# Layer 0's second-block attention on one Trainium2 core: context and latent units taken in turns

## The chip, the cores and the metric

The kernel runs on one core of one Trainium2 chip. The metric is the device time of one execution, in microseconds (us). The engines are TensorE (PE; its weight loads are listed apart as PEld), VectorE (DVE), ScalarE (ACT), GpSimd (POOL) and SyncE (SP), which issues most of the DMAs. Before the change the median of three runs is 2735.27 us (2731.71 to 2745.95).

## The reference, cut to what matters

Two transformer blocks of two layers each follow one another. The change is in the second block, in its layer 0. There two streams of 256 tokens are processed, context and latent. Context queries see the 256 context keys; latent queries see 512 keys, those of the context and their own. In the last layer only the latent stream is needed.

```python
for i in range(DEPTH):
    last = i == DEPTH - 1
    qg_c, kg_c, vg_c, qm_c, km_c, vm_c, pool_c = mixer_inputs(hc, *layer_w, None)
    qg, kg, vg, qm, km, vm, pool_l = mixer_inputs(h, *layer_w, rope)
    mix = token_mix(qg, concat([kg_c, kg]), concat([vg_c, vg]),      # latent: 512 keys
                    qm, concat([km_c, km]), concat([vm_c, vm]), pool_l, ...)
    ...
    if not last:
        mix_c = token_mix(qg_c, kg_c, vg_c, qm_c, km_c, vm_c, pool_c, ...)   # context: 256 keys

def token_mix(qg, kg, vg, qm, km, vm, ...):
    og = attention(qg, kg, vg, HEAD_DIM ** -0.5)     # 6 heads, keys of 64 numbers, 2 key/value heads
    om = attention(qm, km, vm, MLA_QK ** -0.5)       # 6 heads, keys of 96 numbers
    return concat([merge_heads(og), merge_heads(om), op]) @ w_out

def attention(q, k, v, scale):                       # blocks of 128 queries
    p = softmax(einsum(q, k) * scale)
    return einsum(p, v)
```

## The kernel before, in words

Everything is written by hand: each engine has its own instruction list, and semaphores tie the lists together. There is no scheduler; the order of the code is the order on each engine.

The attention of the second block is cut into units. A unit is one stream, one head and one of two tiles of 128 queries, so layer 0 has 2 x 12 x 2 = 48 units and layer 1 has 24. `units(i)` lists them, and unit n of the list is what every engine means by n. In layer 0 the list holds the 24 units of the context stream first, and then the 24 of the latent stream. In each stream the first 12 units are of the heads with keys of 64 numbers (GQA below; their scores are L2463), the last 12 of those with 96 (MLA; L2465).

A unit runs through the engines like this:

- PE, `scores(n)`: one matmul of 128 queries against 256 keys (context) or 512 keys (latent), in float32. Score banks are four (`SCORE_BANKS`), taken in turns by n.
- DVE: the row maximum of the scores (L2925), and its negative, scaled (L2926).
- ACT: the exponential with the sum of each row (L2715).
- DVE: the reciprocal of that sum (L2932), and the product with the probabilities (L2933).
- PE, `turn(n)`: transposes of the probabilities, two pieces of 128 x 128 for a context unit and four for a latent one (L2477).
- ACT: the copy of the transposed probabilities out of the bank (L2724).
- PE, `attend(n)`: probabilities times values, two matmuls for a context unit and four for a latent one (L2494).
- DVE, after every fourth unit: four units (two heads, two tiles) fill one output bank, 6 or 7 in turns, and a copy brings it to `h` (L2939).

The work is staggered. In step n, PE issues `scores(n)`, `turn(n-2)` and `attend(n-3)`. ACT does the exponential of unit n and then the copy of unit n-2. DVE does the maximum of unit n, the normalisation of unit n-1, and where a group of four has ended at unit n-3, its copy. The first `attend` of a group waits (`av_out`) until the bank that it takes has been emptied by the copy of the group before the last.

Before the attention stand the projections of the MLA heads, whose last copies (L2705) the third unit's scores wait for. Behind it stands the output projection (L2515), whose first matmul waits for the last copy to `h`.

A line such as `128x256 f32 x2` in the profile is one float32 matmul: it shows as two records of PE.

Of the kernel before, what the change touches and what calls it, by code (L numbers as in the profile page):

```python
# [1894 lines left out]
GQ, KVH = 6, 2  # L1895
MH, NOPE, ROPE_D = 6, 64, 32
# [99 lines left out]
def build_second(nc, ctx, a, scratch, store, out):  # L1996
# [83 lines left out]
    def streams(i):  # L2080
        return (CTX, LAT) if i < DEPTH - 1 else (LAT,)
# [6 lines left out]
    def cols(s, t=0, n=T):  # L2088
        return slice(s * T + t, s * T + t + n)
# [8 lines left out]

    def units(i):

        return [(s, hd, t) for s in streams(i) for hd in range(GQ + MH) for t in range(2)]

    def layer_ends(i):
        for x in signals:
# [54 lines left out]
    def unit_base(i):  # L2159
        return len(units(0)) if i else 0  # L2160
# [45 lines left out]
    def tensor_program(pe):  # L2206
# [137 lines left out]
        for i in range(DEPTH):  # L2344
# [95 lines left out]
            for t in range(4):  # L2440
# [3 lines left out]
                last.then_inc(*((used_kv.sem, 1) if t == 3 else mla_done.up()))  # L2444

            us = units(i)

            def scores(n):
# [32 lines left out]
            def attend(n):  # L2481
                s, hd, t = us[n]
                if n == 0:
                    pe.wait_ge(*mla_evac.at(i, 2 * MH + 4))
                pe.wait_ge(*pt_ready.at(0, ub + n + 1))
                pair = n // 4
                if n % 4 == 0 and pair >= 2:
                    pe.wait_ge(*av_out.at(0, ub // 4 + pair - 1))
                hi = slice((hd % 2) * HD, (hd % 2 + 1) * HD)
                nk = (T if s == CTX else TT) // P  # L2490
                for k in range(nk):
                    kv = hd // (GQ // KVH)
                    v = vg[:, k, kv * HD:(kv + 1) * HD] if hd < GQ else vm[:, k, (hd - GQ) * HD:(hd - GQ + 1) * HD]
                    last = mm(ps[6 + pair % 2][hi, t * P:(t + 1) * P], v, probT[:, n % 2, k * P:(k + 1) * P],  # L2494
                              start=(k == 0), stop=(k == nk - 1))
                last.then_inc(*av_done.up())

            for n in range(len(us) + 3):
                if n < len(us):
                    scores(n)  # L2500
                if 2 <= n < len(us) + 2:
                    turn(n - 2)
                if n >= 3:
                    attend(n - 3)
# [41 lines left out]
    def scalar_program(act):  # L2546
# [69 lines left out]
        for i in range(DEPTH):  # L2616
# [82 lines left out]
            for t in range(4):  # L2699
# [5 lines left out]
                go(vm[:, t, :], ps[4 + t][:, 0:MH * HD], ACT.Copy).then_inc(*mla_evac.up())  # L2705

            us = units(i)
            for n in range(len(us) + 2):
                if n < len(us):
# [40 lines left out]
    def vector_program(dve):  # L2750
        v = nc.vector

        def step(i, instruction, signal):

            instruction.then_inc(*signal.up())
            dve.wait_ge(*signal.now(0))
# [83 lines left out]
        for i in range(DEPTH):  # L2840
# [78 lines left out]
            for n in range(len(us) + 3):  # L2919
                if n < len(us):  # L2920
                    s, hd, t = us[n]
                    nk = T if s == CTX else TT
                    dve.wait_ge(*sc_done.at(0, ub + n + 1))
                    m1 = smx[:, n % 4:n % 4 + 1]
                    step(0, v.tensor_reduce(m1, ps[SCORE_BANKS[n % 4]][:, 0:nk], AX_X, ALU.max), sm_max)  # L2925
                    v.tensor_scalar(m1, m1, -((HD if hd < GQ else MQK) ** -0.5), None, ALU.mult  # L2926
                                    ).then_inc(*sm_max.up())
                if 1 <= n <= len(us):
                    b = (n - 1) % 4
                    nk = T if us[n - 1][0] == CTX else TT  # L2930
                    dve.wait_ge(*sm_act.at(0, ub + n))
                    step(0, v.reciprocal(ssum[:, b:b + 1], ssum[:, b:b + 1]), sm_norm)  # L2932
                    v.tensor_scalar(prob[:, b, 0:nk], prob[:, b, 0:nk], ssum[:, b:b + 1], None,  # L2933
                                    ALU.mult).then_inc(*sm_norm.up())
                if n >= 3 and (n - 3) % 4 == 3:
                    s, hd, t = us[n - 3]
                    pair = (n - 3) // 4
                    dve.wait_ge(*av_done.at(0, ub + n - 2))
                    v.tensor_copy(h[:, hd // 2, cols(s)], ps[6 + pair % 2][:, 0:T]).then_inc(*av_out.up())  # L2939
            first_low(MlpTiles(i, streams(i)[0]))  # L2940
# [121 lines left out]
    @block.vector  # L3062
    def _(dve):
        nc.vector.memset(ones_row[:, 0:P], 1.0).then_inc(*placed.up())
        nc.vector.memset(ones_row[:, P:], 1.0).then_inc(relu_done.sem, 1)
        vector_program(dve)
# [33 lines left out]
```

## Time and profile before

| what | us |
|---|---|
| median of three runs | 2735.27 |
| lowest, highest run | 2731.71, 2745.95 |
| profiled execution | 2742.86 |
| its span from first to last instruction | 2740.9 |
| PE busy | 2630.0 (96%) |
| DVE busy | 1700.7 (62%) |
| ACT busy | 1028.4 (38%) |

The profile shows one execution. Its time is the span and 2 us around it. The shares are means over a span with many stages: PE is busy nearly all the time, and yet its time depends on the clock that it was granted and on what it works on. The attention of layer 0's second block stands at 1765 to 1883 us of the span. PEclk is the clock granted to TensorE, as a share of 2.4 GHz: 1.00 is 2.4 GHz and 0.50 is 1.2 GHz.

### The profile page before, as it was taken

What the parts mean: (1) busy time and instruction counts of PE and PEld (TensorE: products, weight loads), DVE (VectorE), ACT (ScalarE), POOL (GpSimd) and SP (SyncE); (2) the same over time, 40 slices, a digit from 0 to 9 for tenths busy, and PEclk for the clock granted to TensorE, in tenths of its full rate; (3) what the DMA queues carried; (4) which work ended last, traced back from release to release, by engine and by line L of the source; (5) the groups of instructions that cost most, each with busy time, mean ns of one, the idle gap of its engine ahead of it and who ended that gap; (6) DMA issues with size and microseconds to landing.
All of it is one profiled execution on the core that took longest, in us unless ns stands there. A gap on an engine that the chain in (4) does not pass through costs nothing. (4 is left out here: it accounts for less than half of the span.)

```text
span 2740.9 us, 44687 instructions
## 1 busy us (share of the span) xinstructions
PE 2630.0 (96%) x18787; PEld 2324.0 (85%) x18787; DVE 1700.7 (62%) x2283; ACT 1028.4 (38%) x1275; POOL 99.2 (4%) x179
## 2 busy tenths in 40 slices
PE   8999989999989999989999999999999999989999
PEld 7999888989989999779899954355799899737999
DVE  6887655768768877656678822553455455354555
ACT  4335302444343354204443321643333333264333
POOL 2110000001101100000001000000000000000000
PEclk9999989999999999989999999889999999999999
DMA  8775201647766764004557752100355555210452
GB/s 277 261 260 185 93 1 47 200 140 244 261 216 223 264 224 154 16 1 138 171 174 258 260 193 77 46 1 31 127 183 183 199 184 185 78 62 31 140 183 93
DMA packets 279510, 415.63 MB, mean 152 GB/s; under 512 B 10105, under 2 KB 235721, under 8 KB 277698
## 3 DMA queue, kind: packets, MB, share of 16 engines
q1 hardware_dynamic: 260332, 348.16, 38.5%
q0 software_dynamic: 18128, 64.20, 6.8%
q8 instruction: 112, 1.84, 0.3%
q10 hardware_dynamic: 902, 1.15, 0.1%
q14 instruction: 36, 0.29, 0.0%
HBM read 399.82 MB, written 13.65 MB: 151 GB/s over the span
## 5 line engine op out<-in xcount | busy, mean ns | idle before, releaser
L614 PE MATMUL ps<-h_high,w_high 128*128 128x256 f32 x1984 | 567.9, 286 | 17.5 <-DVE w_low L1407 10.5
L616 PE MATMUL ps<-h_high,w_low 128*128 128x256 f32 x2016 | 572.3, 284 | 0.0
L614 PEld LDWEIGHTS ps<-h_high,w_high 128*128 128x128 f32 x1984 | 382.8, 193 | 20.3 <-DVE w_low L1407 11.4
L616 PEld LDWEIGHTS ps<-h_high,w_low 128*128 128x128 f32 x2016 | 389.0, 193 | 0.0
L1407 DVE TENSOR_TENSOR w_low<-ring,w_high 128x2048 fp32r<-128x2048 f32 x132 | 302.3, 2290 | 138.5 <-ACT w_high L1150 138.2
L615 PE MATMUL ps<-h_low,w_high 128*128 128x256 f32 x1312 | 373.4, 285 | 0.0
L2797 DVE TENSOR_TENSOR w_low<-ring,w_high 128x2048 fp32r<-128x2048 f32 x96 | 220.0, 2292 | 240.6 <-ACT w_high L2581 240.4
L1150 ACT ACTIVATE w_high<-ring 128x2048 fp32r<-128x2048 f32 x132 | 252.3, 1915 | 266.7 <-DMA ring<-in_ffn_w_in 147.9
L2581 ACT ACTIVATE w_high<-ring 128x2048 fp32r<-128x2048 f32 x96 | 183.8, 1916 | 331.2 <-PE ps L2260 304.1
L615 PEld LDWEIGHTS ps<-h_low,w_high 128*128 128x128 f32 x1312 | 254.0, 194 | 0.0
L1428 DVE SCALAR_TENSOR_TENSOR mod_acc<-wmod,cond,mod_acc 128x512 f32<-128x512 f32 x336 | 230.8, 748 | 0.0
L2258 PE MATMUL ps<-h_high,w_high 128*128 128x256 f32 x768 | 218.3, 284 | 2.8 <-DVE h_low L2766 2.8
L2260 PE MATMUL ps<-h_high,w_low 128*128 128x256 f32 x768 | 218.1, 284 | 0.0
L2259 PE MATMUL ps<-h_low,w_high 128*128 128x256 f32 x768 | 218.0, 284 | 0.0
L2258 PE MATMUL ps<-act_high,w_high 128*128 128x256 f32 x768 | 217.5, 283 | 0.0
L2259 PE MATMUL ps<-act_low,w_high 128*128 128x256 f32 x768 | 217.3, 283 | 0.0
L2260 PE MATMUL ps<-act_high,w_low 128*128 128x256 f32 x768 | 217.3, 283 | 0.0
L614 PE MATMUL ps<-act_high,w_high 128*128 128x256 f32 x704 | 200.3, 285 | 0.0
L615 PE MATMUL ps<-act_low,w_high 128*128 128x256 f32 x704 | 199.5, 283 | 0.0
L616 PE MATMUL ps<-act_high,w_low 128*128 128x256 f32 x704 | 199.5, 283 | 0.0
L1383 DVE TENSOR_TENSOR w_low<-ring,w_high 128x2048 fp32r<-128x2048 f32 x64 | 146.3, 2291 | 81.6 <-ACT w_high L1097 80.8
L615 PE MATMUL ps<-w_high 128*128 128x256 f32 x544 | 153.9, 283 | 0.0
(426 smaller groups left out, 5395.0 us busy)
## 6 DMA issues: line engine op xcount, KB each, us to landing
ring<-in_w_mlp SPq DMA_DIRECT2D x96, 1024.0 KB, 5.5
ring<-in_ffn_w_in SPq DMA_DIRECT2D x88, 1024.0 KB, 8.8
wmod<-in_w_mod POOLq DMA_DIRECT2D x96, 512.0 KB, 6.3
ring<-in_ffn_w_out SPq DMA_DIRECT2D x44, 1024.0 KB, 5.1
ring<-in_w_mix_in SPq DMA_DIRECT2D x26, 1024.0 KB, 5.5
ring<-in_xattn_w_kv SPq DMA_DIRECT2D x16, 1024.0 KB, 5.3
mod_scratch<-mod_acc POOLq DMA_DIRECT2D x24, 512.0 KB, 5.5
ring<-mod_scratch SPq DMA_DIRECT2D x12, 1024.0 KB, 6.8
```

Source lines behind the costliest of these rows:

```text
L614: mm(dst, w_hi, x_hi, start=start, stop=False, **more)
L615: mm(dst, w_hi, x_lo, start=False, stop=False, **more)
L616: return mm(dst, w_lo, x_hi, start=False, stop=stop, **more)
L1150: go(w_high[buffer], ring[:, tiles.slot(r, b), :], ACT.Copy).then_inc(w_high_ready.sem, 1)
L1383: v.tensor_tensor(w_low[:, n % RING, :], slot(n), w_high[COLUMN_HIGHS[c]], ALU.subtract).then_inc(*column_low.up())
L1407: v.tensor_tensor(w_low[:, slot, :], ring[:, slot, :], w_high[buffer], ALU.subtract).then_inc(w_low_ready.sem, 1)
L1428: v.scalar_tensor_tensor(mod_acc[:, c, :], w, col, mod_acc[:, c, :], ALU.mult, ALU.add).then_inc(mod_step.sem, 1)
L2258: mm(dst, w_hi, x_hi, start=start, stop=False, **more)
L2259: mm(dst, w_hi, x_lo, start=False, stop=False, **more)
L2260: return mm(dst, w_lo, x_hi, start=False, stop=stop, **more)
L2581: go(w_high[parity], ring[:, tiles.slot(r, q), :], ACT.Copy).then_inc(w_high_ready.sem, 1)
L2797: v.tensor_tensor(w_low[:, slot, :], ring[:, slot, :], w_high[parity], ALU.subtract).then_inc(w_low_ready.sem, 1)
```

## The change

`units(i)` now runs over heads and tiles outside and over the streams inside. In layer 0 the list becomes context, latent, context, latent, and so on: unit 0 is the context's first tile of head 0, unit 1 the latent's. Four units of one stream still share an output bank, but they are now every other unit: groups end at units 8g+6 (context) and 8g+7 (latent). The context's groups always take bank 6 and the latent's bank 7. Layer 1 has one stream, and its order and its banks come out as before.

```diff
     def units(i):
 
-        return [(s, hd, t) for s in streams(i) for hd in range(GQ + MH) for t in range(2)]
+        return [(s, hd, t) for hd in range(GQ + MH) for t in range(2) for s in streams(i)]
+
+    def group_of(i, n):
+
+        both = len(streams(i))
+        return n // (4 * both) * both + n % both
+
+    def first_of_group(i, n):
+        return n % (4 * len(streams(i))) < len(streams(i))
+
+    def last_of_group(i, n):
+        both = len(streams(i))
+        return n % (4 * both) >= 3 * both
...
-                pair = n // 4
-                if n % 4 == 0 and pair >= 2:
+                pair = group_of(i, n)
+                if first_of_group(i, n) and pair >= 2:
                     pe.wait_ge(*av_out.at(0, ub // 4 + pair - 1))
...
-                if n >= 3 and (n - 3) % 4 == 3:
+                if n >= 3 and last_of_group(i, n - 3):
                     s, hd, t = us[n - 3]
-                    pair = (n - 3) // 4
+                    pair = group_of(i, n - 3)
                     dve.wait_ge(*av_done.at(0, ub + n - 2))
                     v.tensor_copy(h[:, hd // 2, cols(s)], ps[6 + pair % 2][:, 0:T]).then_inc(*av_out.up())
```

The lines below are instructions in the order of their engine: line, operation, output and inputs, size, and how many in a row. The lines of the changed kernel are 12 higher. First TensorE in the GQA part. Before, among the context's units:

```order
L2463 MATMUL ps<-qk 128x256
L2477 MATMUL ps<-consts_sb,prob 128x128 x2
L2494 MATMUL ps<-probT,vg 64x128 x2
L2463 MATMUL ps<-qk 128x256
L2477 MATMUL ps<-consts_sb,prob 128x128 x2
L2494 MATMUL ps<-probT,vg 64x128 x2
```

and among the latent's, 60 rows on:

```order
L2463 MATMUL ps<-qk 128x512
L2477 MATMUL ps<-consts_sb,prob 128x128 x4
L2494 MATMUL ps<-probT,vg 64x128 x4
L2463 MATMUL ps<-qk 128x512
L2477 MATMUL ps<-consts_sb,prob 128x128 x4
L2494 MATMUL ps<-probT,vg 64x128 x4
```

After the change, in the same part:

```order
L2475 MATMUL ps<-qk 128x512
L2489 MATMUL ps<-consts_sb,prob 128x128 x4
L2506 MATMUL ps<-probT,vg 64x128 x2
L2475 MATMUL ps<-qk 128x256
L2489 MATMUL ps<-consts_sb,prob 128x128 x2
L2506 MATMUL ps<-probT,vg 64x128 x4
L2475 MATMUL ps<-qk 128x512
L2489 MATMUL ps<-consts_sb,prob 128x128 x4
L2506 MATMUL ps<-probT,vg 64x128 x2
```

A unit's own work is the same; its neighbours are not. Between two scores now stand the turn of the unit of the same stream two places back and the attend of the other stream: 4 transposes with 2 matmuls, then 2 transposes with 4 matmuls.

Then VectorE around the copies to `h`. Before, among the context's units:

```order
L2933 TENSOR_SCALAR prob<-prob,ssum 128x256
L2925 TENSOR_REDUCE smx<-ps 128x1
L2926 TENSOR_SCALAR smx<-smx 128x1
L2932 RECIPROCAL ssum<-ssum 128x1
L2933 TENSOR_SCALAR prob<-prob,ssum 128x256
L2939 COPY h_sb<-ps 128x256
L2925 TENSOR_REDUCE smx<-ps 128x1
```

After the change:

```order
L2945 TENSOR_SCALAR prob<-prob,ssum 128x256
L2951 COPY h_sb<-ps 128x256
L2937 TENSOR_REDUCE smx<-ps 128x1
L2938 TENSOR_SCALAR smx<-smx 128x1
L2944 RECIPROCAL ssum<-ssum 128x1
L2945 TENSOR_SCALAR prob<-prob,ssum 128x512
L2951 COPY h_sb<-ps 128x256
L2937 TENSOR_REDUCE smx<-ps 128x1
L2938 TENSOR_SCALAR smx<-smx 128x1
```

Two copies now come in consecutive steps, once in eight units, where one came in every fourth. Normalisations of 256 and of 512 columns take turns.

## Rows read from the trace of the kernel before

**Rows 1.** the page, busy time of the engines

```profile
PE 2630.0 (96%) x18787; PEld 2324.0 (85%) x18787; DVE 1700.7 (62%) x2283; ACT 1028.4 (38%) x1275; POOL 99.2 (4%) x179
```

**Rows 2.** stretches of layer 0: us, busy by engine, PEclk, DMA share, GB/s

```profile
1764.57:1767.99 3.42, 1.80 (x10) 0.93 (x9) 2.07 (x9) 1.58 (x5) 0.00 (x0) 1.00 0.47 123
1767.99:1808.94 40.95, 40.95 (x121) 23.54 (x120) 16.74 (x65) 13.26 (x48) 0.00 (x0) 0.50 0.04 16
```

**Rows 3.** timeline (start us, us, engine, line, names, shape), first units

```profile
1764.87 0.48 PE L2463 MATMUL ps<-qk 64*128 64x256 f32 x1
...
1770.76 1.22 PE L2463 MATMUL ps<-qk 64*128 64x256 f32 x2
```

**Rows 4.** timeline, one GQA context unit at the low clock

```profile
1784.83 1.22 PE L2463 MATMUL ps<-ksw,qk 64*128 64x256 f32 x2
...
1785.97 0.69 PE L2477 MATMUL ps<-consts_sb,prob 128*128 128x128 f32 x2
...
1786.59 1.12 PE L2494 MATMUL ps<-probT,vg 128*64 128x128 f32 x4
...
1787.64 1.22 PE L2463 MATMUL ps<-qk 64*128 64x256 f32 x2
```

**Rows 5.** timeline, scores of two MLA context units at the low clock

```profile
1801.13 1.22 PE L2465 MATMUL ps<-km,qm 96*128 96x256 f32 x2
...
1803.76 1.22 PE L2465 MATMUL ps<-km,qm 96*128 96x256 f32 x2
```

**Rows 6.** timeline, MLA context units at the full clock

```profile
1811.87 0.70 PE L2465 MATMUL ps<-km,qm 96*128 96x256 f32 x2
...
1812.60 0.43 DVE L2925 TENSOR_REDUCE smx<-ps 128x1 f32<-128x256 f32 x1 [0.36 <-PE ps L2465]
...
1813.25 0.48 ACT L2715 ACTIVATE prob<-ps,smx 128x256 f32<-128x256 f32 x1 [0.59 <-DVE smx L2926]
...
1813.72 0.38 ACT L2724 ACTIVATE probT<-ps 128x256 f32<-128x256 f32 x1
...
1814.14 0.41 PEld L2494 LDWEIGHTS ps<-probT,vm 128*64 128x64 f32 x4 [0.17 <-ACT probT L2724]
...
1814.73 0.70 PE L2465 MATMUL ps<-km,qm 96*128 96x256 f32 x2
...
1816.45 0.42 DVE L2939 COPY h_sb<-ps 128x256 f32<-128x256 f32 x1
```

**Rows 7.** timeline, GQA latent units at the full clock

```profile
1829.12 1.12 PE L2463 MATMUL ps<-qk 64*128 64x512 f32 x2
...
1830.28 0.69 DVE L2925 TENSOR_REDUCE smx<-ps 128x1 f32<-128x512 f32 x1 [1.18 <-PE ps L2463]
...
1830.76 1.09 PE L2494 MATMUL ps<-probT,vg 128*64 128x128 f32 x8
...
1831.20 0.69 ACT L2715 ACTIVATE prob<-ps,smx 128x512 f32<-128x512 f32 x1 [1.39 <-DVE smx L2926]
...
1831.78 0.29 PEld L2463 LDWEIGHTS ps<-qk 64*128 64x128 f32 x2 [0.17 <-issue]
...
1831.88 0.59 ACT L2724 ACTIVATE probT<-ps 128x512 f32<-128x512 f32 x1
```

**Rows 8.** timeline, the last latent score and the first output projection

```profile
1875.36 1.12 PE L2465 MATMUL ps<-km,qm 96*128 96x512 f32 x2
...
1882.83 5.42 PE L2515 MATMUL ps<-h_sb,ring 128*128 128x512 f32 x12 [0.52 <-DVE h_sb L2939]
```

**Rows 9.** busy us by stretch, layer 1's attention, latent units only

```profile
2454.07:2457.48 3.41, 3.41 (x13) 2.54 (x13) 1.36 (x4) 1.45 (x4) 0.00 (x0) 0.50 0.00 0
```

**Rows 10.** timeline, layer 1, a latent unit at the low clock

```profile
2453.92 1.03 PE L2477 MATMUL ps<-consts_sb,prob 128*128 128x128 f32 x4
...
2454.88 1.97 PE L2494 MATMUL ps<-probT,vg 128*64 128x128 f32 x8
...
2456.78 1.45 PE L2463 MATMUL ps<-qk 64*128 64x512 f32 x2
```

## The prediction

> **What bounds the kernel now.** I read the page's busy times first [rows 1]. PE is busy in 96% of the span, so only what changes PE's time, or makes it idle, can move the end much. DVE and ACT have room.
>
> Then I read the busy time by stretch around the changed place, which is where this case is decided [rows 2]. From 1767.99 to 1808.94 us PE is busy all the time and has a granted clock of 0.50, that is 1.2 GHz. Before that it had 1.00 for 3.42 us in which it was busy for only 1.80 us, waiting for the first softmax. The low clock covers all the GQA units of the context after the first three and about six of its MLA units; behind 1808.94 the remaining context units and the latent ones run at about half these durations [rows 6, 7].
>
> The timeline then gives what a unit costs at each clock. A step of the stagger is score, turn, attend.
>
> - Context, GQA, low clock: 1784.83 to 1787.64 = 2.81 us, of which the score is 1.14, the turn 0.62, the attend 1.05 [rows 4]. PE has no gap.
> - Context, MLA, low clock: 1801.13 to 1803.76 = 2.63 us [rows 5].
> - Context, full clock: 1811.87 to 1814.73 is two units, 1.43 us each [rows 6]. Here PE isn't the only bound: its attend (1814.14) starts when ACT's copy ends (1813.72 + 0.38), and the row names that copy as what released it.
> - Latent, GQA, full clock: 1829.12 to 1831.78 = 2.66 us, attend 1.02 [rows 7].
>
> The whole stretch, from the first score (1764.87 [rows 3]) to the first output projection (1882.83 [rows 8]), takes 117.96 us. About 21 us of it are the low clock's: some 10 GQA units at 2.81 - 1.43 and 6 MLA units at 2.63 - 1.43.
>
> **The change part by part.** No instruction is added or removed; the work of each engine in the stretch is the same. Three things change.
>
> *The output banks.* Each stream now has one bank, so the first attend of a group waits for the copy of the same stream's last group, which ended two units earlier, instead of a group back. DVE makes that copy in the step in which the attend is done, and PE's turn of the next step already waits for a later instruction of DVE, the normalisation. The copy is 0.42 us [rows 6] and lies beside the next score, the shortest of which at full clock (context) keeps DVE waiting longer than that. Cost 0. If the cover were gone it would be 6 groups x 2 streams x 0.42 = 5 us at the very most; I keep nothing below 0.
>
> *The latency of a latent unit at full clock.* PE may issue the score of a latent unit when the attend of the latent unit two places back in the list is over. Followed along the rows [rows 7]: score to maximum 1830.28 - 1829.12 = 1.16; maximum to exponential 0.92; exponential to the copy behind it 0.68; copy to attend 0.59 and 0.04 to 0.05 of semaphore (as 1813.72 + 0.38 to 1814.14 [rows 6]); attend to the next score 1.02. Together 4.42 us. That chain spans two units of the list. Before, two latent units took 2 x 2.66 = 5.32 us of PE, so it was hidden. Now the two are a latent and a context unit, with 2.66 + 1.43 = 4.09 us, so the chain sets the pace: a pair takes 4.42 us, 0.33 more. Could the pair take less than 4.09? A context unit's own chain (2.86 for two units [rows 6]) is now well hidden, and PE's own work in one is perhaps 0.1 to 0.15 below 1.43; this would count only if the latent chain were not there, so the bounds for a pair are 3.95 and 4.42, and I take 4.42, since it is a sum of rows.
>
> *The low clock.* This is the large term. The first steps still wait for the first softmax, with little on PE, as before [rows 2]; I take it that the clock falls there again. Then it matters how long it stays down. What the rows show: with context GQA units alone it never came back, though PE had no gap. With context MLA units alone it came back after about six. In layer 1, with latent units alone, it was low for a mere 3.41 us [rows 9], in which PE did little but a turn of four transposes and an attend of eight records, up to 2456.78 [rows 10]. In the new order each run of turn and attend between two scores is 0.62 + 1.90 us (context turn, latent attend: 2456.78 - 2454.88) or about 1.05 + 1.05. That is between the context's 1.67 and the latent's 2.9, and each run is fenced by scores over only 64 rows, as the context's GQA units were. So the two neighbours bound it: back at once, or not before the MLA units. I take the second, because the runs here are broken by such scores as often as before and half of them are nearly the context's own length; it is a close choice. In the MLA part, where context units alone sufficed, I let the clock come back within the first pair.
>
> A page of the Trainium skill says the opposite. "TensorE: Matmul & The Clock Gate", in the part on the clock gate, has it that sustained matmul activity releases the throttle, and that only idle gaps bring it back. By that rule the busy PE of the new order gets its clock back quickly, which is the second case below. The trace disagrees with the rule as it stands: 40.95 us busy in a stretch of 40.95 us, at 0.50 [rows 2].
>
> The price at the low clock. Latent GQA unit: attend 1.90 [rows 10]; four matmuls more than a context attend cost 0.85, so 0.21 a record; the turn is then 0.62 + 2 x 0.21 = 1.05 (the row has 0.96, partly at full clock); the score has 256 columns more in each of two records, and at 0.21 for 128 columns of one pass pair that is 4 x 0.21 more, 2.00. Together 4.95 (bounds: 4.3 with the score row's 1.45 as it stands, 5.32 as twice the full-clock unit). A pair is 2.81 + 4.95 = 7.76.
>
> The sum:
> - first score to unit 4: before 1770.76 - 1764.87 = 5.89 [rows 3]; now two of the four scores are latent (+0.43 at full clock, 1.16 against 1812.60 - 1811.87; +0.85 at the low) and a turn has four pieces (+0.43): 7.6
> - ten more GQA pairs at 7.76: 77.6
> - first MLA pair, midway between 2.63 + 4.8 at the low clock and 4.42: 5.9
> - ten MLA pairs at 4.42: 44.2
> - the last pair to its latent score, half a pair: 2.1 (DVE and ACT work ahead there)
> - last latent score to the output projection, as before: 1882.83 - 1875.36 = 7.5 [rows 8]
>
> Total 144.9 against 117.96, or +26.9 us. In the terms of the profiled execution that is 2742.9 + 26.9 = 2769.8. This execution is 7.6 us above the median of 2735.27, and the trace doesn't say where. If the 7.6 is a longer low stretch among the context's MLA units, it isn't carried over (the new order is at the low clock there whatever comes later); if it lies elsewhere, it is, and the median would be 2762. I take 2767.
>
> What lies behind the stretch isn't moved: the output projection starts from a full bank of weights in either case, and the DMAs are idle in this stretch (share 0.04 [rows 2]), so nothing new is late.
>
> **The rivals.**
>
> *B, the clock comes back within the first GQA pairs* (not slower). The place is the first latent attend next to a context turn at about 1775 us. Layer 1 speaks for it [rows 9, 10], and the skill's rule; the 25 us of context GQA units that PE filled without it speak against. With one pair at the low clock behind the start: 7.6 + 7.8 + 20 x 4.42 + 2.1 + 7.5 = 113.4, 4.6 less than before; each further low pair adds 3.3. In the profiled execution's terms 2738, by the median 2731 to 2740; I call it 2735. It changes sign against my forecast from the point where fewer than about three pairs are low.
>
> *A2, it comes back somewhere in the middle of the GQA part.* Nothing in the trace excludes it, and the runs of before spread over 14 us. With 4 to 8 low pairs behind the start it is 2745 to 2760.
>
> *C, the clock doesn't fall at all at the start.* 5.9 + 21 x 4.42 + 2.1 + 7.5 = 108.3, so -9.7: 2733 in the profiled execution's terms, 2726 by the median. Against it: the first steps have even more waiting, since the first normalisation is behind a maximum of 512 columns, and layer 1's start lost the clock too [rows 9].
>
> *D, it stays low through the MLA part too.* Ten more pairs at 2.63 + 4.8 instead of 4.42, and the end at the low clock: some 36 us more, 2800 or above. The context MLA units that got it back alone speak against.
>
> *E, the order gains as PE work.* The latent chain is shorter than I sum it, no clock is lost, and a pair costs 3.95: 5.9 + 21 x 3.95 + 9.6 = 98.5, -19.5, about 2720. Nothing in the rows supports both halves at once.
>
> *That the change does nothing* would need the pace of a pair to be the sum of both and the same low stretch; its time lies within B's.
>
> **How the numbers follow.** A 0.50, A2 0.10, B 0.25, C 0.05, D 0.05, E 0.05. The likeliest is A, 2767, with a range of its own of 2758 to 2776 (the price of a low latent unit, and the 7.6 us). The range over the cases runs from 2730 to 2776: it leaves out D, E, most of C and the edges of B and A. A measurement of this kernel can tell about 0.5% from no change, here 13.7 us. Slower by more: A, D and most of A2, 0.63. Faster by more: E and a little of B and C, 0.06. Within: 0.31.
>
> **What would show it.** The granted clock in the stretch behind 1768 us: 0.50 for some 85 us is A, under 20 us is B. The distance between two latent scores: 7.8 us at the low clock, 4.4 at the full. At the full clock the latent attend must be released by ACT's copy (L2736), with PE idle about 0.3 us before it; if its distance is 4.1 and nothing waits, my chain is wrong. DVE's copies to `h` must come in twos with no attend waiting for them. Layer 1's attention should be as before. A clock at 1.00 from the first units on would make the prediction wrong whatever the pace.

## The result, and the profile after

| | before | after |
|---|---|---|
| median of the runs, us | 2740.61 (four runs, 2731.71 to 2746.12) | 2770.93 (four runs, 2769.91 to 2772.32) |
| ratio to before | 1 | 1.0108 (95%: 1.0082 to 1.0135) |
| span of the profiled execution, us | 2740.9 | 2767.9 |
| first score to first output projection in layer 0, us | 117.97 | 144.57 |

The kernel became 1.1% slower in these executions; three of twelve later ones didn't lose this time (last experiment). Of the 27.0 us between the two spans, 26.6 lie in the changed stretch. Here are the busy times and the stretches of the profile after, with the columns of [rows 1, 2]:

```profile
PE 2652.7 (96%) x18787; PEld 2333.8 (84%) x18787; DVE 1700.4 (61%) x2283; ACT 1027.2 (37%) x1275; POOL 99.2 (4%) x179
```

```profile
1763.61:1767.02 3.41, 2.32 (x8) 1.13 (x8) 2.06 (x7) 1.69 (x5) 0.00 (x0) 1.00 0.40 136
1767.02:1852.35 85.33, 85.33 (x244) 47.49 (x244) 29.00 (x96) 24.15 (x71) 0.00 (x0) 0.50 0.02 7
1852.35:1907.80 55.45, 50.15 (x280) 32.03 (x278) 31.02 (x101) 26.30 (x72) 0.00 (x0) 1.00 0.00 1
```

The instruction counts are those of before, and PE is busy for 23 us more with the same work. The middle row says why: 85.33 us without a gap at a granted clock of 0.50 (1.2 GHz), where before had 40.95 [rows 2]. Behind it, at the full clock, PE is idle for 5.3 of 55.45 us.

A pair is a latent and a context unit. The next view is TensorE's timeline of one GQA pair at the low clock, in the kernel after, with one line left out: from a latent score over a context score to the next latent one.

```profile
1783.03 2.07 PE L2475 MATMUL ps<-ksw,qk 64*128 64x512 f32 x2
...
1786.07 1.12 PE L2506 MATMUL ps<-probT,vg 128*64 128x128 f32 x4
1787.12 1.22 PE L2475 MATMUL ps<-qk 64*128 64x256 f32 x2
1788.27 0.69 PE L2489 MATMUL ps<-consts_sb,prob 128*128 128x128 f32 x2
1788.89 1.97 PE L2506 MATMUL ps<-probT,vg 128*64 128x128 f32 x8
1790.79 1.22 PE L2475 MATMUL ps<-qk 64*128 64x512 f32 x1
```

1783.03 to 1790.79 is 7.76 us. The next view is an MLA pair at the full clock, with lines of all engines, many left out:

```profile
1865.79 1.13 PE L2477 MATMUL ps<-km,qm 96*128 96x512 f32 x2
...
1866.95 0.69 DVE L2937 TENSOR_REDUCE smx<-ps 128x1 f32<-128x512 f32 x1 [1.56 <-PE ps L2477]
...
1867.87 0.69 ACT L2727 ACTIVATE prob<-ps,smx 128x512 f32<-128x512 f32 x1 [2.19 <-DVE smx L2938]
...
1868.55 0.59 ACT L2736 ACTIVATE probT<-ps 128x512 f32<-128x512 f32 x1
...
1869.19 1.09 PE L2506 MATMUL ps<-probT,vm 128*64 128x128 f32 x8 [0.40 <-ACT probT L2736]
...
1870.20 1.12 PE L2477 MATMUL ps<-km,qm 96*128 96x512 f32 x2
```

1865.79 to 1870.20 is 4.41 us. Each step of the chain that the prediction followed along [rows 7] is here, and PE stands still for 0.40 us until ACT's copy is done. The waits of the stretch, summed (who waited for whom: us, times, longest), list that wait twice, for the weight load and for the matmul. They list no attend that waits for a copy to `h`.

```profile
PEld ps L2506 <- ACT probT L2736: 8.0, 13, 0.6
PE ps L2506 <- ACT probT L2736: 4.8, 12, 0.4
```

### The profile page after: what moved, and what is told of

It is laid out like the page before. It is cut to its first block and busy times, and to the rows that moved or that the text cites. A ratio compares the mean times of both kernels' runs of the same rounds, so it can differ in the third digit from the quotient of the medians.

```text
span 2767.9 us, 44687 instructions
## 1 busy us (share of the span) xinstructions
PE 2652.7 (96%) x18787; PEld 2333.8 (84%) x18787; DVE 1700.4 (61%) x2283; ACT 1027.2 (37%) x1275; POOL 99.2 (4%) x179
## 3 DMA queue, kind: packets, MB, share of 16 engines
q10 hardware_dynamic: 902, 1.15, 0.1%
```

## The experiments

Every experiment was timed against before on the same chip. "Stretch" is from layer 0's first score (its first matmul) to the first output projection, in the profiled execution. "ACT exchanged" is the exchange of two of ACT's instructions, described below. The last column has the time of a pair for the kernels that take turns, and of a context and a latent unit for the others, all at the full clock unless it says low.

| kernel | median us | ratio (95%) | stretch, us | pair or two units, us, GQA / MLA |
|---|---|---|---|---|
| before, in four comparisons | 2742.78 to 2743.32 | 1 | 117.97 | context 2.81 low / 2.63 low, then 1.43; latent 2.66 / 2.51 |
| changed, start filled | 2739.33 | 0.9982 (0.9964 to 1.0001) | 109.17 | 4.41 / 4.41 |
| before, start filled | 2730.13 | 0.9952 (0.9936 to 0.9967) | 100.68 | 1.58, 2.66 / 1.43, 2.51 |
| latent stream first | 2726.51 | 0.9950 (0.9922 to 0.9978) | 99.72 | 1.58, 2.66 / 1.43, 2.51 |
| before, one bank per stream | 2744.97 | 1.0002 (0.9976 to 1.0027) | 117.94 | as before |
| changed, 128-row scores | 2734.80 | 0.9979 (0.9962 to 0.9995) | 107.57 | 4.41 / 4.41 |
| before, 128-row scores | 2723.48 | 0.9926 (0.9910 to 0.9943) | 96.72 | 1.43, 2.51 / 1.43, 2.51 |
| changed, 128-row scores from unit 8 | 2741.17 | 1.0009 (0.9988 to 1.0029) | 118.07 | 4.41 / 4.41 |
| changed, start filled, ACT exchanged | 2732.59 | 0.9956 (0.9939 to 0.9972) | 101.65 | 4.23 / 3.95 |
| changed, ACT exchanged | 2761.51 | 1.0029 (0.9986 to 1.0071) | 100.12 | 4.23 / 3.95 |
| latent first, ACT exchanged | 2727.65 | 0.9947 (0.9930 to 0.9963) | 99.68 | 1.58, 2.66 / 1.43, 2.51 |
| changed, again, 12 executions | 2773.36 | 1.0088 (1.0052 to 1.0123) | 144.56 | 7.76 low / 4.41 |

**The start filled.** Where PE waits for the first softmax, it gets three matmuls that nothing reads.

```diff
+                if i == 0 and n in (2, 3):
+                    pe.wait_ge(*mla_evac.at(i, 2 * MH + 3))
+                    for _ in range(2 if n == 2 else 1):
+                        mm(ps[6][:, 0:TT], ones, qk[:, 3, 0:TT], start=True, stop=True)
                 if 2 <= n < len(us) + 2:
                     turn(n - 2)
```

> The changed order, plus three matmuls of 128 rows by 512 columns that nothing reads, two before layer 0's first turn and one before its second, where TensorE otherwise waits for the first softmax. My theory: the 85 us at the low clock follow from that wait at the start, after which the GQA pairs can't get the clock back; with it filled the clock stays at 1.00, every pair costs 4.4 us, and the stretch from the first score to the output projection takes 108 to 110 us instead of 144.6: about 2735, some 36 below the changed kernel and within 10 of the kernel before. Rival 1 (interleaving costs by itself, by banks, copies or queues): it stays at 2765 or above. Rival 2 (the GQA units lose the clock by themselves, wherever they stand): the clock falls a little later and the time is above 2760.

> The order of before with the same three unread matmuls at the start of layer 0's attention. My theory: the 41 us at the low clock go too, context units cost 1.43 us each from the start, the stretch takes 98 to 100 us instead of 118, and the kernel takes about 2722, some 19 below before. The difference to the changed order with the same filling is then the latent chain alone, 0.33 to 0.47 us a pair or 8 to 11 us. Rival (the low clock belongs to the context's GQA units, which PE fills too thinly for it): the clock falls again within them and the time stays within 5 us of before.

Both got rid of the low clock in the stretch, as expected, and the changed order came out about as forecast (a stretch of 109.17 us for 108 to 110, and 2739.33 for about 2735). The order of before gained less: 2730.13 where about 2722 was expected, 13 us below before and not 19, with a stretch of 100.68 for 98 to 100. Some 1.8 us of that are its GQA context units, twelve at 1.58 us where 1.43 was expected. This is the changed order with the start filled (same columns as above):

```profile
1771.91:1882.00 110.09, 103.30 (x538) 62.02 (x536) 62.10 (x204) 53.37 (x148) 0.00 (x0) 1.00 0.03 10
```

The clock is 1.00 from the first score to the end. The stretch is 35.4 us shorter than in the changed kernel, and the median 31.6 us lower than its 2770.93. All ten executions lay between 2733.78 and 2744.29. Between the two orders with the filling, the stretches differ by 8.5 us: that is what taking turns costs at the full clock.

The single profile alone doesn't show that the filling held the clock up. In it the clock rose to 1.00 at 1771.91, 1.15 us before the first score (1773.06); in the changed kernel's profile it rose at 1763.61, 0.27 us before it (1763.88). Call these an early and a late rise. The profile of the exchange alone, further down, has an early rise as well and kept the clock without filling. What does show it is the times: no filled execution of the changed order (ten of ten) was above 2745, against nine of twelve unfilled ones above 2770; and all ten filled ones of the order of before were below 2735, against 50 of 77 unfilled ones above 2741.

**The streams exchanged**, in the order of before.

```diff
-        return [(s, hd, t) for s in streams(i) for hd in range(GQ + MH) for t in range(2)]
+        return [(s, hd, t) for s in streams(i)[::-1] for hd in range(GQ + MH) for t in range(2)]
```

> The order of before with the two streams exchanged: all latent units first, then all context units. My theory: the wait at the start still drops the clock, but latent units alone get it back within about 4 us, as in layer 1, and the context's units then begin at the full clock and keep it: stretch 99 to 102 us, time about 2724. Rival (context GQA units are at the low clock wherever they stand): the clock falls when they begin, stretch 115 us or more, no gain. A second rival, that the low clock comes from what stands before the attention: as long as before.

The time came as expected, by another way: the clock didn't fall at the start at all in the profiled execution, although PE waits 1.80 us for the first softmax there too. It had risen 0.27 us before the first score (1769.47), as in before (1764.57 and 1764.87 [rows 2, 3]), so these two profiles start alike.

```profile
1769.20:1869.00 99.80, 97.31 (x529) 60.64 (x528) 62.18 (x204) 52.20 (x146) 0.00 (x0) 1.00 0.03 11
```

The same context GQA units that took 2.81 us [rows 4] now take 1.58, so they are not slow in themselves. All seven executions lay within 2722.03 to 2728.76. This is the fastest kernel of the study that computes the reference, by a one-line edit of before.

**One bank per stream, and nothing else of the change.**

```diff
-                if n % 4 == 0 and pair >= 2:
-                    pe.wait_ge(*av_out.at(0, ub // 4 + pair - 1))
+                bank = 6 + (s if i == 0 else pair % 2)
+                if n % 4 == 0 and pair >= (1 if i == 0 else 2):
+                    pe.wait_ge(*av_out.at(0, ub // 4 + pair - (0 if i == 0 else 1)))
...
-                    last = mm(ps[6 + pair % 2][hi, t * P:(t + 1) * P], v, probT[:, n % 2, k * P:(k + 1) * P],
+                    last = mm(ps[bank][hi, t * P:(t + 1) * P], v, probT[:, n % 2, k * P:(k + 1) * P],
...
-                    v.tensor_copy(h[:, hd // 2, cols(s)], ps[6 + pair % 2][:, 0:T]).then_inc(*av_out.up())
+                    v.tensor_copy(h[:, hd // 2, cols(s)], ps[6 + (s if i == 0 else pair % 2)][:, 0:T]).then_inc(*av_out.up())
```

> The order of before with the change's banks alone: in layer 0 all context groups take bank 6 and all latent groups bank 7, so that each group's first attend waits for the copy of the group just before. My theory: the copy of 0.42 us lies beside the next score, so nothing moves: stretch 118 us give or take the low clock's own spread, ratio to before 0.997 to 1.003. Rival (the banks cost something): 10 groups wait up to 0.5 us each, 2 to 5 us more, and the trace shows attends waiting for the copies to h.

The stretch is 117.94 against 117.97 us, the low stretch 40.95 as before, and no attend waited for a copy to `h`. The banks cost nothing.

**Scores over 128 rows.** The score's two operands take all partitions instead of the head's 64. The selection of the head is left out, so these kernels don't compute the reference: they show times only.

```diff
-                    key = qk[hi, 3, 0:nk] if same else ksw[hi, 0:nk]
-                    last = mm(bank[:, 0:nk], qk[hi, hd // 2, q], key, start=True, stop=True)
+                    key = qk[:, 3, 0:nk] if same else ksw[:, 0:nk]
+                    last = mm(bank[:, 0:nk], qk[:, hd // 2, q], key, start=True, stop=True)
```

> The changed order with GQA scores that contract over all 128 partitions instead of the 64 of the head, in both layers; it leaves the selection of the head out, so those scores are of other numbers, and the same size. TensorE's times stay. My theory as the prediction put it: the scores over 64 rows that fence every turn and attend are what the GQA pairs lack; with 128 rows the clock comes back within the first few pairs, the low stretch is under 20 us instead of 85, the stretch to the output projection about 112 to 118 us, the kernel 30 us below the changed one. Rival: rows don't matter and the length of turn and attend without a score between does; then the low stretch stays at about 85 us and the time at 2771.

> The order of before with the same 128-row GQA scores (the selection of the head left out). My theory: the context's GQA units, which stayed at the low clock for 25 us in before, now get it back within a few units; low stretch under 15 us instead of 41, stretch to the output projection 102 to 107 us instead of 118. Rival (only turn and attend without a score between count, and a context unit's are short): as before, 41 us.

The low stretch is gone, but not in the way expected: in both profiled executions the clock was at 1.00 from the first score on, so it did not have to come back. The stretches, 107.57 and 96.72 us, are shorter than the 112 to 118 and 102 to 107 that were forecast, and the changed order is 36 us below the changed kernel where 30 was expected. In the changed order:

```profile
1764.90:1872.90 108.00, 96.78 (x530) 61.50 (x528) 62.24 (x204) 52.83 (x147) 0.00 (x0) 1.00 0.03 11
```

In this profile the clock had risen 0.18 us before the first score (1765.23 and 1765.41), and PE waited 1.09 us for the first softmax, as in the changed kernel: a late rise again, and this time no fall. (The other profile has an early rise, 1.06 us before the first score, and says nothing on this.) That left open whether 128-row scores bring the clock back or only keep it. So the next one uses them from unit 8 on alone:

```diff
+                    if i == 0 and n >= 8:
+                        hi = slice(0, P)
                     key = qk[hi, 3, 0:nk] if same else ksw[hi, 0:nk]
```

> The changed order; layer 0's GQA scores contract over 128 partitions from unit 8 on only (the selection of the head left out there), while units 0 to 7 have their 64. With 128 rows from the start the clock never fell, so that didn't show whether it comes back. My theory: it falls at the start as in the changed kernel, units 4 to 7 run at the low clock, and it comes back within two pairs after unit 8, that is 15 to 35 us after the first score instead of 88; stretch 114 to 124 us. Rival (rows only keep a clock that is up and bring none back): low until the MLA part, stretch 142 to 145 us.

The clock fell and came back (stretches by clock, then the first score with 128 rows in PE's timeline):

```profile
1770.05:1793.95 23.90, 23.90 (x69) 13.52 (x70) 8.04 (x28) 7.28 (x23) 0.00 (x0) 0.50 0.06 25
1793.95:1884.90 90.95, 81.99 (x454) 52.24 (x453) 52.15 (x170) 43.73 (x120) 0.00 (x0) 1.00 0.00 1
```

```profile
1790.11 1.22 PE L2477 MATMUL ps<-qk 128*128 128x256 f32 x2
```

This score comes 20 us after the fall, and the clock was up 3.84 us later; in the same order with 64 rows the low clock lasted 85 us. The times of all ten executions, 2736.70 to 2747.00, lie well under 2770.

**ACT's two instructions exchanged.** In each step ACT copies the transposed probabilities of unit n-2 (L2724) before it takes the exponential of unit n (L2715).

```diff
             for n in range(len(us) + 2):
+                if n >= 2:
...
+                    go(probT[:, b, 0:nk], ps[2 + b][:, 0:nk], ACT.Copy).then_inc(*pt_ready.up())
                 if n < len(us):
...
                        ).then_inc(*sm_act.up())
-                if n >= 2:
...
-                    go(probT[:, b, 0:nk], ps[2 + b][:, 0:nk], ACT.Copy).then_inc(*pt_ready.up())
```

> The changed order, the start filled as in the first experiment, and ACT's two instructions of a step exchanged in both layers: it copies the transposed probabilities of unit n-2 before it takes the exponential of unit n. My theory of the full-clock pace: the copy behind the exponential is in the chain that sets 4.41 us a pair; ahead of it, the chain is cut and the pair falls to PE's own work, 4.1 to 4.25 us in the GQA part and 3.9 to 4.0 in the MLA part. Stretch 101 to 104 us instead of 109.2. Rival (the pace is PE's or DVE's, not that chain's): 109 us. A second rival: the exponential comes later, so the normalisation does, and PE waits at the turn instead; no gain.

> Latent units first, then context units, with ACT's copy ahead of the exponential in both layers. My theory: latent units don't wait for the copy, so nothing there; context MLA units at 1.43 us are held by the same chain over two units and fall to about 1.35, so the stretch goes from 99.7 to 98 or 99 us and the kernel is the fastest of all, about 2725. Rival (the exchange delays the exponential and so the turn): 1 to 3 us slower than latent first alone.

> The changed order with ACT's copy ahead of the exponential, and nothing else. If the low clock and the latent chain are two separate terms, the chain matters only at the full clock: GQA pairs at the low clock stay at 7.76 us (PE without a gap), MLA pairs fall from 4.41 to 3.95, 11 x 0.46 = 5 us: stretch 139.5 us, kernel about 2766. Rival (they aren't separate, the exchange moves the low stretch as well): anything below 135 or above 145 us.

With the start filled the pair fell from 4.41 to 4.23 us (GQA) and 3.95 (MLA), and the stretch from 109.17 to 101.65. PE's latent attend, with the exchange:

```profile
1851.07 1.09 PE L2506 MATMUL ps<-probT,vm 128*64 128x128 f32 x8
```

The wait of 0.40 us is gone, and 3.95 is 1.43 + 2.51 and 0.01, 4.23 is 1.58 + 2.66 less 0.01: PE's own work. So the latent chain is shown. With latent first the exchange did nothing: context MLA units stayed at 1.43, where I had expected 1.35. In that timeline the copy ends at 1851.81 + 0.38 = 1852.19, the attend that needs it starts 0.94 us later and no longer names it as releaser, and score follows score after 1.43 us all the same:

```profile
1851.81 0.38 ACT L2715 ACTIVATE probT<-ps 128x256 f32<-128x256 f32 x1 [0.44 <-PE ps L2477]
...
1852.28 0.30 PEld L2465 LDWEIGHTS ps<-km,qm 96*128 96x128 f32 x2 [0.17 <-issue]
...
1853.13 0.41 PEld L2494 LDWEIGHTS ps<-probT,vm 128*64 128x64 f32 x4 [0.17 <-issue]
...
1853.71 0.30 PEld L2465 LDWEIGHTS ps<-km,qm 96*128 96x128 f32 x2 [0.17 <-issue]
```

So 1.43 us is PE's own, and the copy in [rows 6] merely ended at the moment when PE was ready for it.

The third of them, the exchange alone, surprised. Its profile had no low stretch in the attention at all (stretch 100.12 us), though its instructions at the start and PE's wait of 1.09 us are those of the changed kernel. What differs is when the clock rose: at 1770.94, 1.16 us before the first score (1772.10). This is the low stretch just ahead of the rise:

```profile
1767.53:1770.94 3.41, 3.41 (x7) 2.00 (x6) 2.20 (x6) 0.69 (x2) 0.00 (x0) 0.50 0.00 0
```

Its ten executions fell in two bunches: four at 2726.41 to 2731.96 with a mean clock (granted clock over the whole execution) of 0.976 to 0.979, six at 2760.63 to 2768.36 with 0.962 to 0.965. The profile is of the lower bunch. The upper, with a median of 2763.3, is roughly where I expected the kernel (2766). Against the changed kernel's upper bunch (2773.2, below) it gains 10 us where I forecast 5; no execution of it was profiled, so whether the exchange also shortens the low stretch stays open. Next, the changed kernel was run again as it is.

> The changed kernel itself, unchanged, in more executions. With ACT's exchange the executions fell into two bunches, 2726 to 2732 us at a mean clock of 0.977 and 2761 to 2768 at 0.965, and the profiled one of the first bunch had no low stretch at the start of layer 0's attention. My theory: whether the clock falls at the start differs from one execution to the next; when it doesn't, the changed kernel takes the time of the filled start, 2734 to 2744 us at a clock of 0.976 or more, in about four of ten executions, and nothing lies between 2748 and 2765. Rival: the changed kernel loses the clock always, and all executions lie at 2766 to 2776 us like the first four.

Three of twelve executions lay at 2738.05 to 2740.21 us (mean clock 0.976 to 0.977), nine at 2770.25 to 2777.46 (0.961 to 0.965), none between. With the first four it is 3 of 16. Before has two bunches as well, over its 77 executions in these four comparisons: 27 at 2728.69 to 2736.27 with a median of 2732.7, and 50 at 2741.26 to 2750.76 with 2745.3. If the bunches of the two kernels answer to each other, the change costs 7 us where the clock isn't lost at the start (2739.7 against 2732.7, medians of the lower bunches), and 28 where it is (2773.2 against 2745.3). That they do is argued from the mean clocks and the profiles of the upper bunches; no execution of the lower bunch of either was profiled.

The profiles together show what goes with the fall. In all five in which the clock fell (before, one bank, the changed kernel twice, 128 rows from unit 8), it had risen 0.26 to 0.30 us before the first score. Only one profile has 64-row scores, context first and an unfilled start, and kept the clock: the exchange alone, with its rise at 1.16 us. With latent first (both profiles) and in the changed order with 128 rows from the start, the clock stayed after a rise as late as in the five. All three filled profiles have the early rise.

## Why the prediction was right

It said 2767 us, with 2758 to 2776 for its likeliest case (chance 0.50); measured were 2770.93 and 2773.36. Its steps, one by one:

- *No work added.* Right: the counts are equal.
- *The output banks, cost 0.* Right, shown by the experiment with the banks alone.
- *The low clock stays until the MLA part.* Right: 85.33 us, "some 85" was forecast, and it came back in the first MLA pair (at 1852.35; the pair begins at 1849.20). The filled start shows that this is the term: with it the median is 31.6 us lower.
- *Why it stays.* The prediction compared the length of a turn and attend with the 64-row scores on either side and called it a close choice. The 128-row scores from unit 8 on decide it for the scores: the same runs of turn and attend, and the clock back after 3.84 us. Which property of them matters, the rows or the other numbers that they multiply, is not shown. The choice itself rested on a likeness between rows, at 0.50 against 0.25 for the opposite; that it came out was in part luck.
- *It falls again at the start, as before.* Right for 13 of 16 executions, and wrong as a certainty. Rival C, which I gave 0.05, fits what three executions did; C said 2726 to 2733, they took 2738 to 2740. C's stretch of 108.3 us was near the 109.17 of the filled start. But the four profiles with 64-row scores and the early rise reach the first score at 1772.1 to 1773.5 us, the seven with the late rise at 1763.9 to 1769.5, so an execution that keeps the clock here may have lost some us ahead of the attention; the three were not profiled. The early or late rise goes with the fall, as said above; what makes it early or late wasn't tried.
- *The latent chain.* Right in mechanism and total: 4.42 summed, 4.41 measured, PE waiting for ACT's copy 0.40 us a pair. (One slip in words: the attend in the chain is that of the latent unit four places back in the list from the score that follows it, not two; the sum is the same.) Its price against before was mis-sized in the GQA part: I took the context unit at full clock for 1.43 us from MLA rows; GQA ones take 1.58, so a GQA pair pays 0.17 and an MLA pair 0.47. Twelve of each give 7.7 us, against 8.5 between the two filled kernels.
- *A context unit is held by its own chain at 1.43.* Wrong: it is PE's own work. It changed nothing in the sum.

The sum of the prediction against the trace: start 7.6, measured 7.72; ten low pairs 77.6 and 77.60; the first MLA pair 5.9 and 5.43; ten MLA pairs 44.2 and 44.12; half a pair 2.1 and 2.34; the end 7.5 and 7.36. Together 144.9 and 144.57; the errors are small and partly cancel.

*Layer 1 as before.* Nearly: its attention took 63.36 us against 64.95, first score to first output projection. In before the clock was low for 3.41 us inside it [rows 9], here it had been low just ahead of it. The order of before with the start filled has 63.37 too, so this isn't the change's.

*The 7.6 us above the median.* I took about half of it off, since no row said where it lay. The profiled execution of before was of the upper bunch and the median of the three of the lower, so the figure to go by was the sum's own, 2769.8, without the half.

*Rival B* (back within the first pairs) is refuted by the profile. The Trainium skill, in the clock-gate part of "TensorE: Matmul & The Clock Gate", says that activity releases the throttle. This case's trace disagrees for 85.33 us of PE without a gap; it agrees for the kernel whose scores had 128 rows from unit 8 on.

## What to carry to other kernels

A stretch in which PE is busy all the time can still run at half its clock, and what stands in the order decides how long. Look at the granted clock by stretch before counting instructions, and try first the work that kept or regained the clock elsewhere in the trace. When two kinds of work are taken in turns, sum the chain of the longer kind over the distance to its next unit: what was hidden behind two long units may not be hidden behind a long and a short one. And compare executions in bunches by their mean clock, since a single profile shows only one of them; before two profiles are compared, see whether the clock stood alike where the changed stretch begins.

## What the runs showed of the hardware that was not expected

- The same program loses the clock at the start of this attention in some executions and not in others: 13 of 16 for the changed kernel, 6 of 10 with ACT exchanged, none of 10 with the start filled, by their times. In the profiles it fell only where it had risen 0.26 to 0.30 us before the first score, after waits of 1.09 us (changed) and 1.62 us (before); after a rise 1.16 us before it, the same wait of 1.09 us cost nothing.
- Once low, the clock stayed so through 85.33 us of TensorE without a gap; with scores over 128 partitions in place of 64, and no other change to the program, it was back 3.84 us after the first of them.
- A unit whose score has 64 rows costs more than one with 96 or 128, at the full clock: a context unit takes 1.58 us with it and 1.43 with the others, a latent unit 2.66 and 2.51. Widening the scores to 128 rows made the stretch of the old order 96.72 us, below the 100.68 of the filled one.
